# State-space matrices made one stage earlier on GpSimd, and VectorE's copies of one of them split in two

## What is computed

```python
def first_block(x, ...):
    for layer in range(DEPTH):                      # DEPTH = 2
        h = h + _token_mixer(_rmsnorm(h, norm1[layer]), ...)   # pooling and attention
        h = h + _conv_ffn(_rmsnorm(h, norm2[layer]), ...)      # the "network"
    return _rmsnorm(h, norm_f)

def s5(u, a_re, a_im, log_dt, b_re, b_im, c_re, c_im, d_skip, w_glu, b_glu):
    ...
    bb_re = coef_re * br - coef_im * bi
    bb_im = coef_re * bi + coef_im * br
    ...                                             # a complex recurrence over the tokens
    y = einsum(s_re, c_re) - einsum(s_im, c_im) + d_skip * uf
```

## Time and profile before

| | us |
|---|---|
| median of 3 runs | 1575.78 |
| lowest and highest | 1575.41, 1576.16 |
| the profiled execution, device time | 1577.53 |
| its span in the profile | 1575.7 |

### The profile page before, as it was taken

One profiled execution on the slowest core, in us unless ns is written; L12 is line 12 of the kernel. 1 busy time (PEld: TensorE's weight loads), 2 busy tenths in 40 slices (PEclk: granted clock), 3 DMA queues, 4 the chain that ended last, 5 costly groups with the idle time before them and its releaser, 6 DMA issues.

```text
span 1575.7 us, 24893 instructions
## 1 busy us (share of the span) xinstructions
PE 1517.7 (96%) x10700; PEld 1384.9 (88%) x10700; DVE 1099.5 (70%) x1175; ACT 780.7 (50%) x886; POOL 460.4 (29%) x288
## 2 busy tenths in 40 slices
PE   6999999999999996999999999989999998999997
PEld 5799999988888996999988879988888897888886
DVE  6546766698756545766788756876988558688863
ACT  5333554565544323554666446454765454466542
POOL 1202400145406784300145651101455000025510
PEclk9999999999999998999999999999999999999999
DMA  6574334455455634355655444334555544245552
GB/s 248 187 267 175 120 143 177 178 188 186 179 194 187 254 141 181 111 217 197 226 185 188 157 146 168 127 108 153 186 186 180 182 145 152 95 173 187 187 181 86
DMA packets 44697, 272.96 MB, mean 173 GB/s; under 512 B 4875, under 2 KB 10251, under 8 KB 15404
## 3 DMA queue, kind: packets, MB, share of 16 engines
q1 hardware_dynamic: 44588, 271.38, 48.1%
HBM read 262.97 MB, written 8.39 MB: 172 GB/s over the span
## 4 chain that ended last, share of the span: by engine, by line
PE 83%; POOL 6%; DVE 5%; ACT 2%; DMA 2%; issue 1%; SPq 0%; DVEq 0%; ACTq 0%; POOLq 0%
PE gemm L540 31%; PE gemm L511 28%; PE aux L540 15%; POOL s_made L1989 2%; DVE w_lo L1335 2%; POOL s_cw L1989 2%; DMA raw<-in_weights 2%; PE gemm L616 1%; POOL pool_w L1989 1%; ACT w_hi L985 1%; PE aux L597 1%; PE aux L562 1%; PE gemm L924 1%; PE aux L511 1%; PE aux L626 1%
## 5 line engine op out<-in xcount | busy, mean ns | idle before, releaser
L1335 DVE TENSOR_TENSOR w_lo<-raw,w_hi 128x2048 fp32r<-128x2048 f32 (+3 forms) x248 | 570.3, 2301 | 237.6 <-ACT w_hi L985 235.0
L985 ACT ACTIVATE w_hi<-raw 128x2048 fp32r<-128x2048 f32 (+3 forms) x248 | 460.6, 1858 | 355.4 <-PE gemm L511 204.3
L511 PE MATMUL gemm<-x_two,w_hi 128*128 128x256 f32 x1952 | 359.9, 287 | 0.0
L511 PEld LDWEIGHTS gemm<-x_two,w_hi 128*128 128x128 f32 x1952 | 308.4, 194 | 2.6 <-issue 1.9
L511 PE MATMUL gemm<-x_two,w_lo 128*128 128x256 f32 x976 | 278.2, 285 | 0.0
L540 PE MATMUL gemm<-x_two,w_hi 128*128 128x512 f32 x672 | 234.6, 399 | 0.0
L1989 POOL TENSOR_TENSOR tmp<-tmp 128x512 f32<-128x512 f32 x24 | 35.7, 1486 | 565.4 <-ACT tmp L1011 565.3
L511 PEld LDWEIGHTS gemm<-x_two,w_lo 128*128 128x128 f32 x976 | 189.1, 194 | 0.0
L540 PE MATMUL gemm<-y_two,w_hi 128*128 128x512 f32 x528 | 185.5, 396 | 0.0
L540 PE MATMUL gemm<-x_two,w_lo 128*128 128x256 f32 x672 | 174.9, 281 | 0.0
L2109 POOL TENSOR_TENSOR cv<-cv,rstd 128x512 f32<-128x512 f32 x44 | 116.6, 2650 | 177.8 <-ACT cv L1066 177.8
(11 more groups left out here) (359 smaller groups left out, 2731.1 us busy)
## 6 DMA issues: line engine op xcount, KB each, us to landing
raw<-in_weights SPq DMA_DIRECT2D x224, 1024.0 KB, 4.8
raw<-in_weights SPq DMA_DIRECT2D x16, 768.0 KB, 4.2
bias_table<-tab SPq DMA_DIRECT2D x3, 1024.0 KB, 5.3
bm<-bias_table SPq DMA_DIRECT2D x8, 384.0 KB, 6.1
raw<-in_weights SPq DMA_DIRECT2D x4, 576.0 KB, 3.7
s_inputs<-s_made SPq DMA_DIRECT2D x1, 2048.0 KB, 7.3
s_outputs<-s_cw SPq DMA_DIRECT2D x1, 2048.0 KB, 8.5
s_v<-s_inputs SPq DMA_DIRECT2D x1, 2048.0 KB, 9.5
```

Of the source, the lines that this page charges most:

```text
L511: mm = pe.matmul(out, lhs, rhs, start=fresh and m == 0, stop=end and m == 2, skip_group_check=True)
L985: me.give(act.activation(w_hi[i % SPL][:, 0:n], raw[i % RAW][:, 0:n], ACT.Copy), w_hi_ready)
L1335: me.give(v.tensor_tensor(w_lo[i % RAW][:, 0:n], raw[i % RAW][:, 0:n], w_hi[i % SPL][:, 0:n].bitcast(F32), ALU.subtract), w_lo_ready)
```

## The change

GpSimd makes the input matrices directly behind its last work for `ffn(0)`, in front of the sum of squares that belongs to the second mixer. SyncE waits for them behind M1's load in place of M11's, and for the output matrices behind M15's in place of M18's. VectorE, in front of the second layer's attention, now waits until the output matrices have been stored (`cw_out`). VectorE's copies of the input-output matrices stand in two halves behind the splits of E9 and E10, in place of all behind the split of E7.

```diff
@@ SyncE, behind weights(i)
-                if i == first("v", 1) + 11:
+                if i == first("v", 1) + 1:
                     sp.wait_ge(v_made, 1)
                     load(v_dram, s5_made.rearrange("p r g c q n -> p (r g c q n)"), v_out)
                     load(s5_bc[:, :, :, :], a["s5_c"], s5c_in)
-                if i == first("v", 1) + 18:
+                if i == first("v", 1) + 15:
                     sp.wait_ge(cw_made, 1)
                     load(cw_dram, s5_cw.rearrange("p r t c n -> p (r t c n)"), cw_out)
@@ VectorE, mixer(layer), in front of attention
                 me.take(u_zero)
+                if layer:
+                    v.wait_ge(cw_out, 16)
@@ VectorE, called between the splits of ffn(1)'s down projection
             def s5_within(k):
-                if k != 4:
+                if k not in (6, 7):
                     return
-                me.take(k_psum)
-                me.give(v.memset(s5_k[:, :, :, :, :], 0.0))
-                me.settle()
-                for q in range(4):
+                if k == 6:
+                    me.take(k_psum)
+                    me.give(v.memset(s5_k[:, :, :, :, :], 0.0))
+                    me.settle()
+                for q in ((0, 1), (2, 3))[k - 6]:
                     rows = slice(32 * q, 32 * q + 32)
                     ins = v.tensor_copy(s5_k[rows, :, :, q, :], A[rows, 0:BANK].rearrange("p (g d n) -> p g d n", g=4, d=T5))
-                me.give(ins, k_kept)
+                if k == 7:
+                    me.give(ins, k_kept)
@@ GpSimd
                 if layer:
                     sum_squares()
                     ffn(0)
+                    me.settle()
+                    s5_inputs()
                     sum_squares()
                 else:
                     g.wait_ge(tab_ready, GROUPS)
                 me.give(g.memset(ub[:, :, :], 0.0), u_zero)
                 if layer:
-                    s5_inputs()
                     s5_outputs()
```

## The result

The changed kernel takes **1554.15 us** (median of 4 runs, 1553.18 to 1555.20), the kernel before on the same chip 1575.60 us: a ratio of 0.9867, 95% interval 0.9855 to 0.9880. The forecast was 1555.4 us, with a range of 1553.5 to 1561.0. By the ratio the gain is 21.0 us, where 20.4 had been summed. The profiled execution took 1553.18 us, its span 1551.4.

A forecast was written before the change was run, and what follows sets the result against it. TensorE was taken to bound the kernel; removing its two waits, with their clock loss, was to save 15.3 + 5.06 = 20.4 us, from 1577.53 to 1557.1 profiled, a median of 1555.4 us; range 1553.5 to 1561.0.

The follow-up runs named there:

- e8: Kernel before, with SyncE's wait for the output matrices moved from M18's to M21's load, VectorE's to before M22, and the s_k copies split: 1554.12 us.
- e6: Changed kernel with twelve more GpSimd operations in front of the input matrices (first triple repeated four times more, same result): 1567.28 us.

## What to carry to other kernels

When a wait goes back through several engines, ask which of them stands still in order: it was not the late matrices that cost 13.7 us but the DMA queue that stood in front of two weight loads for them, and moving that one wait behind three more loads gained 13.9 us, most of what re-planning 90 us of another engine's work did (with the split copies beside it, all but a wait of 1.4 us: `e8`). Place side work on a busy engine behind an instruction whose result is wanted soon, never in front of it, and look at the first engine that is late in turn; whether it stands in one piece or two matters less. If work is moved beside another engine's, cost both engines' loss and count every small operation there, not only the large ones.

## What the runs showed of the chip

- GpSimd's operations and VectorE's operations with two inputs from SBUF take turns, and the loss falls on both. While the input matrices ran, GpSimd lost 14.7 us (43.7 against 29 alone) and VectorE 10.7 (30.7 against 20.0). The Trainium skill, "SBUF — State Buffer", who interferes with whom, has the second to issue block until the first finishes, and the trace agrees, one operation at a time:

```profile
446.39 1.29 POOL L1993 TENSOR_TENSOR s_made<-s_made,pool_w 128x512 f32<-128x512 f32 x1
447.76 2.98 POOL L1993 TENSOR_TENSOR s_made<-s_made,s_st 128x512 f32<-128x512 f32 x1
446.61 3.22 DVE L1335 TENSOR_TENSOR w_lo<-raw,w_hi 128x2048 fp32r<-128x2048 f32 x1 [2.33 <-ACT w_hi L985]
```

The split starts at 446.61, under a GpSimd operation that ends at 447.68. It takes 3.22 us in place of 2.29, so 0.93 us of standing, until 447.54. GpSimd's next operation takes 2.98 in place of 1.05 us, so 1.93 of standing, until 449.69; the split ends at 449.83. So a split costs GpSimd nearly its own length once (the eight splits are 17.4 us long alone, GpSimd lost 14.7), and it costs VectorE what is left of the GpSimd operation in flight. A small `x_two` mostly stands behind such an operation (1.31 in place of 0.48 us at 435.95) and costs GpSimd less than 0.1 us.
- A 2 MB store from SBUF took 11.0 us at 470 and 11.7 us at 549, between weight loads, where the same stores had taken 7.3 and 8.5 us before, and a 1 MB load behind the first landed 11 us after its issue, against 4.8 us for the median load. A store costs the loads around it even where its own end is wanted by nobody.
- TensorE's clock can fall from 1.00 to 0.50 (from 2.4 to 1.2 GHz) after a wait, and the price is not proportional to the wait, nor the same each time. Behind the wait of some 13.7 us the first scores and the next block took 1.9 to 2.8 us more than at full clock in four traces; behind the one of 3.6 us it was 0.1 to 2.6 us in five. And the slow stretch can lie under a later wait and cost next to nothing: in `e6` 13.1 us of lateness cost 13.4.
